# Where the split weights lie in SBUF, modulo 256 bytes, relative to the activations they are multiplied with

## What is computed

```python
for l in range(DEPTH):                      # first block, DEPTH = 2
    z = rms_norm(x, norm_mix[l]) @ w_in[l]          # 1024 -> 2560
    x = x + concat(attention, hgrn2, conv)(z) @ w_out[l]
    h = rms_norm(x, norm_mlp[l])
    x = x + jnp.square(jax.nn.relu(h @ w_mlp_in[l])) @ w_mlp_out[l]   # 1024 -> 4096 -> 1024
for l in range(DEPTH):                      # second block
    mix = gated linear attention (l = 0) or dilated attention (l = 1), and attention over `mem`
    x = _layer_norm(DN_ALPHA * x + mix @ w_out[l])
    f = _peer(x, ...)                       # 16384 experts, top 16 of 8 heads
    x = _layer_norm(DN_ALPHA * x + f)
```

## The kernel before

| class | before |
|---|---|
| column-wise with x | 192 |
| row-wise with x | 64 |
| row-wise with HH or AH | 0 |
| with MEMH, both ways | 0 |

## Time and profile before

### The profile page before, as it was taken

The page is one execution under the profiler, slowest core; times in us unless marked ns, Lnnn a source line. Parts: engine busy times, 40 slices in busy tenths (PEclk is TensorE's granted clock), DMA queues, the critical chain, the costliest instruction groups (busy, mean ns, idle before and its releaser), DMA issues.

```text
span 2753.2 us, 45677 instructions
## 1 busy us (share of the span) xinstructions
PE 2676.4 (97%) x18520; PEld 2435.3 (88%) x18520; DVE 1707.2 (62%) x2680; ACT 1374.2 (50%) x1713; POOL 191.4 (7%) x130
## 2 busy tenths in 40 slices
PE   8989999899999999999999999999999999999997
PEld 7869889699898999999999888988999999999886
DVE  5646556465455899745555565566899645555665
ACT  5555443654354568644444444444568544444442
POOL 0210000400001600000000000002500000000000
PEclk9999999999999999999999999999999999999999
DMA  5315552155535436756565675524356755565672
GB/s 217 108 66 213 188 213 93 62 187 189 186 135 192 152 135 248 287 196 222 200 225 199 234 270 198 188 77 144 135 183 245 274 200 214 206 221 211 231 263 87
DMA packets 74411, 515.99 MB, mean 187 GB/s; under 512 B 8272, under 2 KB 8544, under 8 KB 18592
## 3 DMA queue, kind: packets, MB, share of 16 engines
q1 hardware_dynamic: 58576, 424.70, 43.3%
q0 software_dynamic: 10208, 43.45, 4.5%
q10 hardware_dynamic: 5488, 45.91, 4.0%
HBM read 474.19 MB, written 39.85 MB: 187 GB/s over the span
## 4 chain that ended last, share of the span: by engine, by line
PE 87%; DVE 9%; ACT 2%; issue 1%; DMA 1%; POOL 1%; ACTq 0%; DVEq 0%; POOLq 0%
PE lin L1589 17%; PE lin L1591 17%; PE lin L1590 17%; PE m L1589 9%; PE m L1591 8%; PE m L1590 8%; PE m L2126 4%; DVE lo L957 1%; PE m L1708 1%; POOL w L1531 1%; PE m L1729 1%; PE m L2025 0%; PE m L2105 0%; PE m L1741 0%; DVE x L1188 0%
## 5 line engine op out<-in xcount | busy, mean ns | idle before, releaser
L957 DVE TENSOR_TENSOR lo<-raw,hi 128x2048 fp32r<-128x2048 f32 x357 | 818.0, 2297 | 657.7 <-ACT hi L447 656.6
L447 ACT ACTIVATE hi<-raw 128x2048 fp32r<-128x2048 f32 x403 | 769.3, 1912 | 482.7 <-PE m L1591 342.8
L1589 PE MATMUL lin<-xh,hi 128*128 128x256 f32 x3376 | 964.6, 286 | 14.7 <-DVE lo L957 7.3
L1590 PE MATMUL lin<-xl,hi 128*128 128x256 f32 x3376 | 944.0, 280 | 0.0
L1591 PE MATMUL lin<-xh,lo 128*128 128x256 f32 x3376 | 944.0, 280 | 0.0
L1589 PEld LDWEIGHTS lin<-xh,hi 128*128 128x128 f32 x3376 | 636.5, 189 | 23.7 <-DVE lo L957 8.8
L1590 PEld LDWEIGHTS lin<-xl,hi 128*128 128x128 f32 x3376 | 635.7, 188 | 3.6 <-issue 1.0
L1591 PEld LDWEIGHTS lin<-xh,lo 128*128 128x128 f32 x3376 | 635.9, 188 | 0.0
L1589 PE MATMUL m<-hi,ah 128*128 128x512 f32 x1024 | 400.4, 391 | 0.0
L1591 PE MATMUL m<-hi,al 128*128 128x512 f32 x1024 | 399.0, 390 | 0.0
L1590 PE MATMUL m<-lo,ah 128*128 128x512 f32 x1024 | 398.2, 389 | 0.0
(11 more groups left out here) (358 smaller groups left out, 2935.2 us busy)
## 6 DMA issues: line engine op xcount, KB each, us to landing
raw<-stream SPq DMA_DIRECT2D x403, 1024.0 KB, 4.8
gate_table<-stg ACTq DMA_DIRECT2D x16, 2048.0 KB, 10.7
g<-gate_table POOLq DMA_DIRECT2D x32, 1024.0 KB, 8.2
rows<-rows ACTq DMA_DIRECT2D x4, 1024.0 KB, 6.9
memh<-mem_turned_scratch POOLq DMA_DIRECT2D x3, 1024.0 KB, 5.3
meml<-mem_turned_scratch POOLq DMA_DIRECT2D x3, 1024.0 KB, 8.9
x_scratch<-x ACTq DMA_DIRECT2D x2, 1024.0 KB, 4.2
x<-x_scratch ACTq DMA_DIRECT2D x2, 1024.0 KB, 6.8
```

Source lines behind the costliest of these rows:

```text
L447: act.activation(HI[i % SLOTS][:], RAW[:, i % SLOTS, :], ACT.Copy).then_inc(hi_ready, 1)
L957: dve.tensor_tensor(LO[i % SLOTS][:], RAW[:, i % SLOTS, :], HI[i % SLOTS][:].bitcast(F32), ALU.subtract).then_inc(lo_ready, 1)
L1589: pe.matmul(out_, ah, bh, start=first, stop=False, **kw)
L1590: pe.matmul(out_, ah, bl, start=False, stop=False, **kw)
```

## The change

The buffers `HI` and `LO` get starts of their own, and the region `mix0` is moved with them. `HI_PLACE` and `LO_PLACE` only keep the buffers from overlapping.

```diff
+LINE = 256
+HI_OFF = [64, 64, 64, 64]
+HI_PLACE = [0, 1, 2, 3]
+LO_OFF = [0, 128, 192, 32]
+LO_PLACE = [0, 2, 3, 1]
...
         RAW = at("raw", [P, SLOTS, HP])
-        HI = [at(f"hi{i}", [P, HP], F32R) for i in range(SLOTS)]
-        LO = [at(f"lo{i}", [P, HP], F32R) for i in range(SLOTS)]
-        cursor[0] += 64
+        base = (cursor[0] + LINE - 1) // LINE * LINE
+        HI = [at(f"hi{i}", [P, HP], F32R, off=base + 4 * HP * HI_PLACE[i] + HI_OFF[i]) for i in range(SLOTS)]
+        base += 4 * HP * SLOTS + LINE
+        LO = [at(f"lo{i}", [P, HP], F32R, off=base + 4 * HP * LO_PLACE[i] + LO_OFF[i]) for i in range(SLOTS)]
+        cursor[0] = base + 4 * HP * SLOTS + LINE
         XH = at("xh", [P, KT, TOK], F32R)
         XL = at("xl", [P, KT, TOK], F32R)
...
         X = at("x", [P, TT, D])
+        cursor[0] = (cursor[0] + LINE - 1) // LINE * LINE + 64
         mix0 = cursor[0]
```

## The result

The changed kernel takes 2772.3 us in the median of 3 runs (2768.4 to 2775.6), the kernel before 2752.4. The ratio is 1.0069, with a 95% interval of 1.0052 to 1.0085: slower, by some 0.7%, where the forecast was 2739 us. The profiled execution took 2768.4 us with a span of 2766.2, so its span is 13.0 us longer than that of the earlier trace rows; it was the shortest of the three, and I account for these 13.0 us.

The account below looks back on a forecast made before the run. TensorE, busy in 97% of the span, was taken as the bound through distances between matmuls. Terms -28 + 3 + 7 + 4 + 1 = -13 us took the profiled 2755.3 to 2742, forecast median 2739 us, range 2712 to 2782.

Parts of the forecast that it names:

- The high parts, column-wise: Two of three weight loads per triple go from relation 192 to 64 and the fast distance: 28 us less.
- The prediction's own sign: Its test: wrong if column-wise distance exceeds 118 in two slots or more, or VectorE's growth makes TensorE wait.
- The low parts, column-wise: Third load of each triple, relation 0, 128, 192, 32 by slot: 3 us more, from slot 0.
- the mixture: Column-wise triples with two relations pay for changes between them: 2 ns per triple, 7 us more; bounds 0 and 47.
- The experts' output and the MLP's second product: 1,280 matmuls with a moving low part leave relation 0: 4 us more, bounds 0 and 8; high parts unchanged.
- The rest: Row-wise with x: 256 columns 1 us more, 512 columns 0; splitting on ScalarE and VectorE: 0.
- The fourth: Rival, chance 0.33: column-wise, each change of relation throws the stream off its step; slower, 2797 us.
- its cheaper variant: Milder case of the fourth rival: column-wise slots 0 and 3 gain, 1 and 2 pay; 2765 us.
- The second: Rival, chance 0.13: stream settles at 113.3 ns column-wise in every slot, the mixture costs nothing; 2714 us.
- The third: Rival, chance 0.14: stream stays slow and classes cancel, or addresses or read ports don't matter; 2752 us.
- the rule of the two read ports: Skill's rule: TensorE's weight loads take no read bandwidth from the running matmul; as applied, places and time change nothing.
- The formula behind the prediction's 109.2 ns: Skill's back-to-back issue gap, N/2.4 + 2.5 ns at 256 columns; 10,128 matmuls at 109.2 would save 87 us.

Follow-up runs that it names:

- e2: Against the changed kernel, all LO buffers start 192 bytes behind a multiple of 256, HI and mix0 staying at 64; 2746.9 us in one run.
- e1: Against the changed kernel, all LO buffers start 64 bytes behind a multiple of 256, as HI and mix0 do; 2743.5 us, ratio 0.9955.
- e3: Against the changed kernel, HI and mix0 move from 64 to 192 behind a multiple of 256, LO keeping 0, 128, 192, 32; 2771.8 us in one run.
- e4: Against the changed kernel, HI, LO and mix0 all at 192, giving the relations of the kernel before at other addresses; 2750.6 us in one run.
- e12: Against the changed kernel, all LO buffers start at a multiple of 256, HI staying at 64; 2766.6 us in one run.
- e5: Against the changed kernel, LO at 192 in slots 0 and 2 and 64 in slots 1 and 3, HI at 64; 2729.9 us, ratio 0.9911.
- e11: Against the changed kernel, LO at 192 in slot 0 alone and 64 in slots 1 to 3, HI at 64; 2729.3 us, ratio 0.9918.
- e6: Against e2, AL begins 128 bytes further, giving it relation 0 to LO, while HL stays; 2740.9 us, ratio 0.9947.
- e9: Against the changed kernel, HI and mix0 at 192 and LO at 64 in all slots, the mirror of e2; 2761.6 us in one run.

## Why the prediction was wrong

*The high parts, column-wise (28 us less).* The step that failed is "Two of three weight loads of a triple go from relation 192 to 64", each priced by its own relation. The three matmuls of a triple go as one pattern. With the third at 0, 32 or 128 none of them is fast; with it at 192 all three are, the unchanged third too. That e2 gains 30.1 us with the low parts at 192 in all slots, close to the 28, is luck: there all three matmuls gain and not two, but only in about 78% of the blocks of twelve, since 7% were fast before and the `u` panels begin slow. The prediction's own sign was met as well: in the long stretch slots 1 and 3 are over 118 ns, at 118.4 and 119.8, and slot 3 is the slowest, not slot 0.

*The low parts, column-wise (3 more), and the mixture (2 ns per triple, 7 more).* No single cost per change of relation fits. (64, 64, 192) changes twice per triple and is the best set of all; (192, 192, 64) and (64, 64, 0) change as often, and are fast only in part or never. Together the three column-wise terms were 18 us less, and the trace has 4.2 less: slot 2 gives 9.0 us, and the other three slots take 4.9 of it back. Of the 26 us missed in the whole span (13 less expected, 13 more measured), 14 are here.

*The experts' output and the MLP's second product (4 more).* Measured 13.1 + 3.4 = 16.5 more, 12 off, and past the bound of 8. "The 2,560 with the high parts stay at 0" is true of the addresses and false of the times: the high ones rose from 226.5 to 231 with their neighbour. It is the same error. e1 differs from the changed kernel in the low parts alone and gives back all of the 16.5 and 2.3 more; e3 brings 12.0 us with the high parts' relations as before.

*The rest* held: 1.5 us more in the row-wise class of 256 columns for the 1 I took, 0.5 less in that of 512 (89.77 to 89.24 us). VectorE's 2297 and ScalarE's 1912 ns stood still, and the waits stayed short.

*The rivals.* The fourth had the right sign. Its mechanism, a stream thrown off its step by each change, isn't what the runs show, and its cheaper variant named the wrong slots: 2 gains, and the loss lies at 512 columns. The second's 2714 needed the fast pattern everywhere at no cost elsewhere; the nearest that I built is 2729. The third, in which nothing moves, fell by the 30.1 us of e2; its other form, in which the classes cancel, didn't come about either, with 4.2 less against 16.5 more.

*Against the rule of the skill.* Fourteen kernels with the same instructions have spans from 2728.6 to 2771.6 us, and the table above shows where: in the distances between matmuls. The Trainium skill, "SBUF — State Buffer", Who interferes with whom, says that TensorE never waits on anyone. It says this of other engines, and the traces don't speak against that: what they show is that the pace depends on where TensorE's own two operands lie to each other. By the rule of the two read ports, as the prediction applied it, nothing would have moved; there the measurement decides. What in the memory or the array makes it so, no run here shows. The formula behind the prediction's 109.2 ns the Trainium skill gives, in the section named there, for an isolated matmul, and says that a stream with weight loads is paced by both operations; so the 113.3 ns seen here doesn't contradict it.

What is shown: for sets of one relation, the distance goes with the relation and not with absolute addresses (e4); the matmuls of a triple can't be priced one by one (e2, e3, e12); some sets have two or more steady patterns, and the stream keeps the one it comes in with (e1, e5, e11). Why (64, 64, 192) always ends in the fast one, and its mirror doesn't, is open; so is whether the next load or the own operand counts (e6). And since one set can run at several paces, the relations alone don't give a time.

## What to carry to other kernels

Where TensorE is busy all the time, read the distance of starts in each steady stretch by class of operands; if one shape has several distances at one granted clock, the starts of the stationary and the moving operand modulo 256 bytes are worth a trial. Price a repeating group of matmuls as one unit, by a run, not as a sum over its members, and check the other classes that read the same buffer: here the best place for one (LO at 192, column-wise) is the worst for another (AH), and giving each slot what it carries most (e5) or just one pushing slot (e11) took 0.8 to 0.9% off the kernel before. A rule drawn from one layout's stretches, without the set they stood in, isn't enough to choose offsets blind.

## What was not expected of the hardware

- One set of relations can hold several steady distances at one clock: 113.3 and 117.8 ns at 64 alone; 117.4, 118.5 and 120.0 at 96 alone; 117.8 and 122.3 at (64, 64, 0).
- Which one it is repeats: e4 has its three fast column-wise stretches where the kernel before has them, at other addresses.
- The order by size turns with the shape: relation 0 is the fastest seen at 512 columns (226.7 ns) and with 120.0 among the slowest at 256; 64 and 192 are the fastest at 256.
- The 512-column products have several patterns too. Modulo 256 the set (0, 128, 0) is the same in four kernels, and by the starts of the matmuls with HH it ran at 233.5 ns in e2, at 231.1 in e9 and in slot 2 of the changed kernel, and at 229.0 in slots 0 and 2 of e5, each behind a panel at 226.7. In which one it settles, no run explains.
- The weight load itself shows nothing of it: its record lasts 188 to 189 ns in the column-wise classes before and after.
